# Two-layer hybrid decoder trunk: dilated attention with queries sorted by parity, and a last step in two halves

## The reference

```python
h = rms_norm(x);  z = h @ w_in + b_in            # 1024 x 7936 weights
y_a = silu(layer_norm(conv31(a * sigmoid(ga)) + b)) @ a_w_out
# three patterns (window, dilation) = (128, 1), (512, 4), (2048, 16), 4 heads of 64 each:
#   query t sees keys t - j * dilation, j = 0..128; outputs merged by the softmax over their log sums
y_b = merge(...) @ b_w_out
y_c = (gb * conv3(gc * hc)) @ c_w_out
x += (sigmoid(g0) * y_a + sigmoid(g1) * y_b + sigmoid(g2) * y_c) @ w_o
x += cross_attention(rms_norm(x), rms_norm(mem))  # 4 heads of 256
x += swiglu(h) (layer 0, 2816 wide)  or  top-2-of-8 expert swiglu (layer 1, 3584 wide)
```

## Time and profile before

| | us |
|---|---|
| median of 3 runs | 1923.4 (1922.88 to 1925.44) |
| the profiled execution | 1920.78 |
| its span, first to last instruction | 1919.1 |
| TensorE busy in it | 1903.7 |
| VectorE busy | 1543.2 |
| ScalarE busy | 1226.8 |

### The profile page before, as it was taken

The page is one execution under the profiler, slowest core; times in us unless marked ns, Lnnn a source line. Parts: engine busy times, 40 slices in busy tenths (PEclk is TensorE's granted clock), DMA queues, the critical chain, the costliest instruction groups (busy, mean ns, idle before and its releaser), DMA issues.

```text
span 1919.1 us, 27337 instructions
## 1 busy us (share of the span) xinstructions
PE 1903.7 (99%) x10829; PEld 1663.8 (87%) x10830; DVE 1543.2 (80%) x1396; ACT 1226.8 (64%) x1101; POOL 70.3 (4%) x79
## 2 busy tenths in 40 slices
PE   9999999999999999999999999999999999999998
PEld 9989999999999989999988888888888888888886
DVE  7988876575568988864688888888888888888886
ACT  5545755544455454745567777777777777777775
POOL 1000000100000000000000000000000000000000
PEclk9999999999999999999999999999999999999999
DMA  9443554445545444543599999999999999999992
GB/s 337 168 147 132 181 190 158 153 176 191 181 161 196 158 142 165 197 176 132 206 371 381 370 388 368 401 375 373 378 357 411 373 383 385 348 405 376 382 386 108
DMA packets 76985, 521.39 MB, mean 272 GB/s; under 512 B 9440, under 2 KB 9696, under 8 KB 15840
## 3 DMA queue, kind: packets, MB, share of 16 engines
q1 hardware_dynamic: 73328, 508.10, 69.5%
q0 software_dynamic: 2992, 11.01, 2.0%
q10 hardware_dynamic: 576, 1.05, 0.2%
HBM read 512.79 MB, written 7.34 MB: 271 GB/s over the span
## 4 chain that ended last, share of the span: by engine, by line
PE 90%; DVE 5%; ACT 3%; issue 1%; DMA 1%; SPq 0%; ACTq 0%; DVEq 0%
PE psum L1619 20%; PE psum L1621 20%; PE psum L1620 20%; PE psum L1633 14%; PE psum L1634 7%; DVE wlo L1000 2%; ACT whi L544 2%; PE psum L2083 1%; PE psum L1861 1%; PE psum L1841 1%; PE psum L1780 1%; PE psum L1755 1%; DMA raw<-in_stream 1%; DVE U L1023 0%; SPq L367 0%
## 5 line engine op out<-in xcount | busy, mean ns | idle before, releaser
L1000 DVE TENSOR_TENSOR wlo<-raw,whi 128x2048 fp32r<-128x2048 f32 x477 | 1086.6, 2284 | 260.1 <-ACT whi L544 259.8
L544 ACT ACTIVATE whi<-raw 128x2048 fp32r<-128x2048 f32 x477 | 909.7, 1909 | 253.3 <-PE psum L1621 202.4
L1619 PE MATMUL psum<-whi,act_hl 128*128 128x512 f32 (+1 forms) x1472 | 568.1, 386 | 0.9
L1621 PE MATMUL psum<-whi,act_hl 128*128 128x512 f32 (+1 forms) x1472 | 560.6, 381 | 0.0
L1620 PE MATMUL psum<-wlo,act_hl 128*128 128x512 f32 (+1 forms) x1472 | 560.0, 380 | 0.0
L1633 PE MATMUL psum<-h_hl,whi 128*128 128x512 f32 x1216 | 432.7, 400 | 0.3 <-DVE U L1344 0.2
L1634 PE MATMUL psum<-h_hl,wlo 128*128 128x256 f32 x1216 | 340.9, 280 | 0.0
L1619 PEld LDWEIGHTS psum<-whi,act_hl 128*128 128x128 f32 x1472 | 277.3, 188 | 55.6 <-DVE wlo L1000 4.2
L1621 PEld LDWEIGHTS psum<-whi,act_hl 128*128 128x128 f32 x1472 | 277.1, 188 | 53.7
L1620 PEld LDWEIGHTS psum<-wlo,act_hl 128*128 128x128 f32 x1472 | 277.5, 188 | 51.6 <-issue 0.7
L1633 PEld LDWEIGHTS psum<-h_hl,whi 128*128 128x128 f32 x1216 | 228.5, 188 | 58.1 <-issue 2.8
(11 more groups left out here) (259 smaller groups left out, 1432.2 us busy)
## 6 DMA issues: line engine op xcount, KB each, us to landing
raw<-in_stream SPq DMA_DIRECT2D x473, 1024.0 KB, 6.9
raw<-in_stream SPq DMA_DIRECT2D x12, 256.0 KB, 7.3
raw<-in_stream SPq DMA_DIRECT2D x4, 512.0 KB, 3.6
U<-in_stream SPq DMA_DIRECT2D x2, 1024.0 KB, 11.5
xacc<-U POOLq DMA_DIRECT2D x3, 512.0 KB, 6.9
xT<-in_x_cols ACTq DMA_DIRECT2D x4, 256.0 KB, 6.8
memhat<-in_mem_cols SPq DMA_DIRECT2D x1, 1024.0 KB, 16.3
hrow<-U POOLq DMA_DIRECT2D x1, 1024.0 KB, 9.5
```

Source lines behind the costliest of these rows:

```text
L544: act.activation(whi[:, n % SPLIT, 0:words], src[:, 0:words], ACT.Copy).then_inc(hi_ready, 1)
L1000: dve.tensor_tensor(wlo[:, n % SPLIT, 0:words], src[:, 0:words], whi[:, n % SPLIT, 0:words].bitcast(F32), ALU.subtract).then_inc(lo_ready, 1)
L1619: pe.matmul(o, st[0], mv[0], start=start, stop=False, **kw)
L1621: return pe.matmul(o, st[1], mv[0], start=False, stop=stop, **kw)
```

## The change

- Scores are made for all even positions as one block of queries and all odd positions as another. Pattern 1 needs both halves of the keys, patterns 2 and 3 only the keys of the same parity: eight blocks for nine. v of patterns 2 and 3 is made with its tokens in parity order too, by a stationary operand with a step of two; the masks and the turned output are laid out to match.
- Scores of two heads are made together, their products alternating between partitions 0 to 63 and 64 to 127, each head with its own two banks. `HEAD_AT` and the tap tables move.
- The product over `memhat` goes in two halves, at chunks 7 and 8.
- The first chunks arrive in four, two and one transfers.
- The last chunk finishes one bank first; each half of the last rows is split in two single-pass parts (`y_hi`, `y_lo`) and spread with single-pass products. In `finish` the root's argument is prepared early, gain is applied to the first halves before the root is known, and one of four output transfers is issued by ScalarE.

```diff
-HEAD_AT = [10, 13, 16, 19]
-OT_AT = 23
-CONV_C_AT = {17: (0, 1), 20: (2, 3)}
+HEAD_AT = [10, 13, 17, 20]
+GROUP_COL = ((0, 256, 384), (256, 0, 128))
+KEY_BLOCKS = (((0, 0), (0, 1), (1, 0), (2, 0)), ((1, 1), (2, 1), (0, 0), (0, 1)))
+OT_AT = 24
+CONV_C_AT = {16: (0, 1), 19: (2, 3)}
-CONV_A_AT = dict(zip(range(3, 28), (2, 6, 6, 4, 7, 7, 7, 3, 4, 6, 4, 6, 9, 3, 0, 6, 5, 0, 5, 6, 3, 6, 6, 6, 7)))
+CONV_A_AT = dict(zip(range(3, 29), (2, 6, 6, 4, 5, 5, 7, 3, 5, 6, 4, 6, 9, 0, 3, 6, 0, 4, 5, 7, 3, 6, 6, 6, 7, 3)))
-PARTED = 3
+PARTED, PIECES = 3, (4, 2, 1)
...
+        def head_bank(h, b):
+            return bank[4 + 2 * (h % 2) + b][:]
...
-            gp.iota(dist, pattern=[[-1, S]], base=P, channel_multiplier=1).then_inc(const, 1)
+            gp.iota(dist, pattern=[[-1, S]], base=0, channel_multiplier=2).then_inc(const, 1)
+            gp.iota(steps_back, pattern=[[-1, P]], base=0, channel_multiplier=1).then_inc(const, 1)
...
             def head_mask
+                for b in range(TB):
+                    mine(dve.scalar_tensor_tensor(prob[:, b, :], head_bank(h, b), 0.125, mask[:, 256 * b:256 * b + 512],
+                                                  op0=ALU.mult, op1=ALU.add))
                 settled()
+                for b in range(TB):
+                    mine(dve.tensor_reduce(small[:, 2 + b:3 + b], prob[:, b, :], AX.X, ALU.max))
...
                 if n == 6:
                     dve.wait_ge(mrt_ready, 1)
                     mine(dve.reciprocal(rstd[:], rstd[:]))
+                if n in (7, 8):
                     settled()
-                    mine(dve.tensor_tensor(memhat[:], memhat[:], rstd[:].unsqueeze(1).to_broadcast([P, DB, S]), ALU.mult))
+                    some = memhat[:, 4 * n - 28:4 * n - 24, :]
+                    mine(dve.tensor_tensor(some, some, rstd[:].unsqueeze(1).to_broadcast([P, DB // 2, S]), ALU.mult))
...
-                        tok = tuple(a[:, k, P * t:P * t + P] for a in (hi, lo))
+                        tok = tuple(a[:, k, t::TB] if parity else a[:, k, P * t:P * t + P] for a in (hi, lo))
...
+            def scores(lay, p):
+                if p == 0:
...
+                else:
+                    pe.wait_ge(o_ready, 4 * lay + 2)
+                for b in range(TB):
+                    for g in range(GROUPS):
+                        for h in range(2):
+                            q_, k_ = (a[64 * h:64 * h + 64, 2 * g + p, :] for a in (qT, kT))
+                            at = GROUP_COL[b][g]
+                            ins = pe.matmul(head_bank(h, b)[:, at:at + (P if g else S)], q_[:, b::TB],
+                                            k_[:, b::TB] if g else k_, start=True, stop=True)
...
             def last_rows(r):          # ScalarE, r == 0
+                act.wait_ge(wc_ready, NE)
+                for half in range(2):
+                    act.wait_ge(*((w_used, MOE + NE * PER_E) if half else (y_first, 1)))
+                    act.activation(y_hi[:, 512 * half:512 * half + 512], bank[4 + half][:], ACT.Copy, scale=wcur)\
+                       .then_inc(y_hi_s, 1)
             def last_rows(r):          # VectorE, r == 0
+                for half in range(2):
+                    dve.wait_ge(y_hi_s, half + 1)
+                    at = slice(512 * half, 512 * half + 512)
+                    dve.scalar_tensor_tensor(y_lo[:, at], bank[4 + half][:], wcur, y_hi[:, at].bitcast(F32),
+                                             op0=ALU.mult, op1=ALU.subtract).then_inc(y_lo_s, 1)
...
             def finish(r):             # ScalarE
+                for j, (t, half) in enumerate(FINAL_ORDER):      # (0, 0), (1, 0), (0, 1), (1, 1)
+                    act.wait_ge(fo_done, 4 * r + j + 1)
+                    act.activation(fsq[:, j, :], final_bank(t, half), ACT.Square,
+                                   accum_out=small[:, j:j + 1]).then_inc(fo_sq, 1)
+                    if half:
+                        act.wait_ge(fo_sq, j + 1)
+                        act.wait_ge(fo_ms, t + 1)
+                        act.activation(small[:, 6 + t:7 + t], small[:, j:j + 1], ACT.Sqrt, scale=1.0 / D,
+                                       bias=small[:, 4 + t:5 + t]).then_inc(fo_rt, 1)
+                act.wait_ge(fo_own, 4)
+                act.activation(yout[:, 1, 0:512], yout[:, 1, 0:512], ACT.Copy, scale=small[:, 7:8]).then_inc(fo_act, 1)
+                act.wait_ge(fo_act, 1)
+                act.dma_start(out[0, P:2 * P, 0:512], yout[:, 1, 0:512]).then_inc(out_sent, 16)
...
             def finish(r):             # VectorE
                 for t in range(TB):
+                    dve.wait_ge(fo_sq, t + 1)
+                    dve.tensor_scalar(small[:, 4 + t:5 + t], small[:, t:t + 1], 1.0 / D, EPS, ALU.mult, ALU.add)\
+                       .then_inc(fo_ms, 1)
+                    dve.tensor_tensor(yout[:, t, 0:512], final_bank(t, 0), gfin[:, 0:512], ALU.mult).then_inc(fo_own, 1)
+                for t in range(TB):
                     dve.wait_ge(fo_rt, t + 1)
                     dve.reciprocal(small[:, 6 + t:7 + t], small[:, 6 + t:7 + t]).then_inc(fo_own, 1)
+                    dve.wait_ge(fo_own, t + 3)
+                    dve.scalar_tensor_tensor(yout[:, t, 512:D], final_bank(t, 1), small[:, 6 + t:7 + t], gfin[:, 512:D],
+                                             op0=ALU.mult, op1=ALU.mult).then_inc(fo_ready, 1)
+                    if t == 0:
+                        dve.tensor_scalar(yout[:, 0, 0:512], yout[:, 0, 0:512], small[:, 6:7], None, ALU.mult)\
+                           .then_inc(fo_ready, 1)
...
+                def last_down(c, f):
+                    pe.wait_ge(lo_ready, first + PER_E * (NE - 1) + c + 1)
+                    for o in range(2):
+                        for k in range(2):
+                            at = P * (2 + k)
+                            ins = three(bank[4 + o][:], (eT_hi[f % 2][:, at:at + P], eT_lo[f % 2][:, at:at + P]),
+                                        wt(first + c, k, D, 512 * o, 512), False, k == 1)
+                        ins.then_inc((y_first, w_used)[o], 1)
...
+                for half in range(2):
+                    at = slice(512 * half, 512 * half + 512)
+                    pe.wait_ge(y_hi_s, half + 1)
+                    for t in range(TB):
+                        pe.matmul(final_bank(t, half), last_sel[:, P * t:P * t + P], y_hi[:, at], start=False, stop=False,
+                                  skip_group_check=True)
+                    pe.wait_ge(y_lo_s, half + 1)
+                    for t in range(TB):
+                        pe.matmul(final_bank(t, half), last_sel[:, P * t:P * t + P], y_lo[:, at], start=False, stop=True,
+                                  skip_group_check=True).then_inc(fo_done, 1)
```

More of the change, by code:

```diff
@@ L208, in trunk @@
         in_gain = sem("in_gain")
-        in_part = [[sem(f"in_part{n}_{i}") for i in range(3)] for n in range(PARTED)]
+        in_part = [[sem(f"in_part{n}_{i}") for i in range(PIECES[n] - 1)] + [w_raw[n]] for n in range(PARTED)]
         part_hi, part_lo = sem("part_hi"), sem("part_lo")
@@ L350, in trunk, with final_bank @@
         LN_BANK = (5, 6)
+        def head_bank(h, b):
+            return bank[4 + 2 * (h % 2) + b][:]
+        FINAL_ORDER = ((0, 0), (1, 0), (0, 1), (1, 1))
+        def final_bank(t, half):
+            return bank[FINAL_BANK[2 * t + half]][:]
         @block.sync
@@ L364, in _ @@
             for n in range(PARTED):
-                for i in range(4):
-                    words = slice(512 * i, 512 * i + 512)
-                    sp.dma_start(raw[:, n, words], stream[n, :, words]).then_inc((in_part[n] + [w_raw[n]])[i], 16)
+                for i in range(PIECES[n]):
+                    size = CW // PIECES[n]
+                    words = slice(size * i, size * i + size)
+                    sp.dma_start(raw[:, n, words], stream[n, :, words]).then_inc(in_part[n][i], 16)
                 if n == 1:
@@ L1760, in values @@
                 pe.wait_ge(pr_ready, k + 1)
[L1761 to L1765 removed]
+                for b in range(TB):
+                    for j in range(4):
+                        ins = pe.transpose(head_bank(h, b)[:, P * j:P * j + P], prob[:, b, P * j:P * j + P], ident[:])
                 ins.then_inc(pt_done, 1)
@@ L1818, in _ @@
                             weigh(lay, h)
-                    for h in range(HEADS):
-                        if c == HEAD_AT[h] + 1:
-                            scores(lay, h)
+                    for p in range(2):
+                        if c == HEAD_AT[2 * p] + 1:
+                            scores(lay, p)
                     if c == OT_AT + 1:
@@ L2186, in body @@
                                 turn(f, k_e)
-                            down(c + 1, e, f - 1, 1, k_e)
+                            if last and r == 0 and f == FSTEPS:
+                                last_down(c + 1, f - 1)
+                            else:
+                                down(c + 1, e, f - 1, 1, k_e)
```

165 lines of the change are left out of this document (72 added, 93 removed).

## The result

The changed kernel takes 1905.57 us (median of 4 runs, 1904.96 to 1907.18); the kernel before took 1924.18 us (4 runs, 1922.88 to 1925.44) beside it. The ratio is 0.9905, 95% interval 0.9887 to 0.9922: the medians are 18.6 us apart. The forecast was 1910.6 us and 12.8 us; rival 1, whole overlap in the scores, stood at 1907.0 us.

The account below looks back on a forecast made before the run. TensorE, busy 1903.7 of 1919.1 us, was taken as the bound. Terms -2.07 (memory norm), -0.9 (transposes), -1.8 (values), -5.9 (scores), -2.1 (end) sum to -12.8 us from the median 1923.4: 1910.6 us, range 1905.5 to 1915.5.

Parts of the forecast that it names:

- rival 1: Attention scores: weight loads overlap across array halves too, saving 9.5 us for 5.9; 1907.0 us in all; chance 0.25.
- Scores: Attention scores of head pairs: halves alternate but loads queue at 0.111 us each, 2.85 a pair; -5.9 us.
- Values: Attention value products: nine blocks to eight, two fp32 instructions fewer in each of 8 heads; -1.8 us.
- Transposes: Attention: nine blocks to eight, one transpose fewer per head, 8 heads in two layers; -0.9 us.
- Memory norm: Before chunk 9: with memhat's product spread over two later steps, TensorE no longer waits for the weight split; -2.07 us.
- cover of chunk 10: Memory norm: chunk 10's split ends at 70.5, TensorE needs it at 70.95, so 0.4 us of cover.
- Stepped reads: Value chunks and scores: stationary reads with a step of two words cost nothing; bounds up to +19.6 and +10.7 us.
- Rival 4: Value chunks and scores: step-of-two loads cost more; at double the load 1940.9 us; chance 0.08.
- VectorE: Attention stages: VectorE's load becomes about 99.5 us against TensorE's 108, so it stays covered, on average with 8 us.
- rival 3: Attention stages: VectorE becomes the bound, costing 1.6 us a layer; 1915.9 us with chunk 10's cover lost; chance 0.06.
- Opening: Kernel start: one more iota, more mask operations, fewer first-chunk transfers; price 0, bounds -0.8 and +0.5 us.
- The end: After the last expert matmul: shorter chain to the last product, -2.15, with some tenths returned by transfers; -2.1 us taken.

Follow-up runs that it names:

- step four: Changed kernel whose value chunks of patterns 2 and 3 read their stationary tokens with a step of four words (wrong data): 1928.34 us, 1.0029 of the kernel before.

## Why the prediction came out as it did

The sign and most of the mechanisms held; the choice between the scores' rates did not. The time lies 5 us under the forecast, and nearer to rival 1 than to it. It is only 0.07 us inside the range, and that it is inside at all is luck: by the profiles the two kernels are 15.5 us apart, by the medians up to 18.6.

- **Scores, the step that failed: "If loads still queue one behind another, 24 x 0.111 = 2.66 a pair".** They don't queue across halves. A pair's group is 2.01 us; 2.8 was named for the forecast and 1.95 for rival 1. The saving is 4 x (4.32 - 2.01) = 9.2 us for 5.9, so rival 1 had the mechanism and, with 9.5, the price. The row used measured loads in one place of the array, which says nothing about two places; the bound was chosen because it had a row, not because the row bore on the question.
- **Values, mis-sized.** The term counted instructions, 16 x 0.114 = 1.8. The groups measure 2.5. Six of the eight heads' values stood right before scores in the old kernel and stand before weight matmuls now; those six lose 0.34 each, the two that always stood before weight matmuls 0.22, which is the two instructions.
- **Transposes, right:** 8 x 0.11 = 0.9.
- **Not in the sum:** 0.9 to 1.0 us of the attention stages that is in no group; its cause stays open.
- **Memory norm, right.** 2.07 foretold, 2.21 in the trace, 2.20 back when it is undone. The cover of chunk 10 was reckoned from the end of chunk 8's last matmul (65.15) and not from the next start; with starts it is 0.7, not 0.4.
- **Stepped reads, right**, at nothing. Rival 4 had its price right too: a load without cover shows in full, 21.8 us at step four.
- **VectorE, right but for 0.4 us a layer.** The stretch 81 to 190 of the changed kernel:

```profile
81.00:190.00 109.00, 108.84 (x726) 98.77 (x725) 101.61 (x166) 59.15 (x79) 0.00 (x0) 1.00 0.45 159
...
DVE U L1226 <- ACT U L664: 6.6, 10, 1.5
```

It is busy 101.6 of 109.0 us, its longest sum of waits for ScalarE fell from 10.1 to 6.6, as rival 3's "such a wait shrinks" had it, and one chunk a layer, chunk 23, is late: a small piece of rival 3, which had 1.6 a layer. Running those taps later got back 0.84 us in all.
- **Opening, right** at nothing that can be told: -0.27 in the first pair of profiles, but two profiles of before have 44.90 and 44.40, and eleven with the new opening 44.2 to 45.2.
- **The end, mis-sized after its last step.** The chain is 2.5 shorter, a bit more than worked out, but the run ends only 0.4 to 1.2 us earlier (10.51 and 10.84 in two profiles of changed; 11.73 and 11.21 in two of before). The text gave "some tenths" for the last transfers; they took 1.3 or more of the 2.5. Second queue and bytes are excluded. Where the instruction fetch came after the output, in the profile of step four, the stretch was 9.61: 2.1 less than the first profile of before, which is the term of the sum, and the time after the last product was 3.9 us for 3.5, the "some tenths". So what was missing from the term is the fetch that falls among the transfers, 0.9 us or more in the other eight profiles. That rests on one profile without it.
- **Routing was not in the sum.** The low clock there moves a run by 1 to 3 us. At like routing (107.84 before, 107.79 after) the profiled executions are 1922.64 and 1907.15: 15.5 us apart. The medians are 18.6 and 16.6 apart in two sets; the first set's median of before, 1924.18, is 1.0 to 1.5 above the three later ones. Against the forecast's 12.8, the 15.5 hold 3.3 more from the scores, 0.7 more from the values, 0.1 from the memory norm and 0.9 from no group; 0.8 less for chunk 23, and 1.7 less from the end (0.4 in this pair for 2.1). The opening cost 0.8 in this pair, and stretches that the change does not touch gave as much back, up to 0.4 each; they differ so from run to run.

## What to carry to other kernels

When a change puts work into separate parts of a unit, a rate measured in one part bounds that part only: look for a row of the parts together, or leave both ends of the range equally likely. Price a stepped stationary read by the 16-byte pieces that it touches against the pace at which it has to arrive, and expect to pay in full beyond it. A chain shortened at the very end is worth only what the last transfer's landing lets through, so read the wait for the outputs, and whatever else moves over the same engines then, before you count the chain. And compare stages, not only totals: a stage whose clock varies can hide or feign more than the edit under study.

## What the runs showed of the hardware

- fp32 passes of 64 rows in alternating halves: 24 passes in 2.01 us, against 3.46 in turn. Loads of the two halves start 4 to 6 ns apart.
- Values that stand right before scores cost 0.12 us more than the same values before weight matmuls (2.04 and 1.92).
- A stationary read of 128 fp32 words: pace of 0.12 at steps one and two, 0.177 at three, 0.233 at four.
- A 16 KB instruction fetch that starts amid the output transfers: the last one lands 4.3 to 5.2 us after issue, against 3.4 in the one profile where the fetch starts behind them.
- The granted clock in routing differs from execution to execution: 3.4, 6.8 or 10.2 us at half speed, and the stage takes 105.1, about 106.4 or 107.8 us with it.
